# Forgetting attention on one core: cumulative forget terms as stacked high and low rows, three logits banks, longer lags

## The reference, cut to what matters

```python
def forgetting_attention(h, w_in, b_f, w_out):          # 256 tokens, 16 heads of 64
    q, k, v, f_logit = split(h @ w_in)
    log_f = log_sigmoid(f_logit + b_f)                  # one value for each token and head
    c = cumsum(log_f, axis=1)                           # the forget sums
    logits = einsum(q, k) * scale + c[query] - c[key]
    p = softmax(where(key <= query, logits, -inf))      # query blocks of 128
    return einsum(p, v) @ w_out
```

## Time and profile before

| | |
|---|---|
| time, median of 3 runs | 2557.5 us (2547.1 to 2561.46) |
| the profiled execution | 2556.97 us |
| its span | 2555.3 us |
| PE busy / weight loads | 2199.8 us (86%) / 1933.2 us (76%) |
| DVE, ACT, POOL busy | 1588.1, 1111.8, 474.7 us |
| granted PE clock, mean | 0.927 |
| chain that ended last, share of PE | 42%; 12% each for L749, L750, L751 |

### The profile page before, as it was taken

How to read it: one execution, slowest core, us unless ns; L and a number is a source line. 1 busy time by engine, 2 the same in 40 slices (tenths; PEclk the granted TensorE clock), 3 DMA queues, 4 the chain that set the end, 5 groups by cost and what they waited for, 6 DMA issues and landing times.

```text
span 2555.3 us, 40376 instructions
## 1 busy us (share of the span) xinstructions
PE 2199.8 (86%) x15366; PEld 1933.2 (76%) x15376; DVE 1588.1 (62%) x2534; ACT 1111.8 (44%) x1624; POOL 474.7 (19%) x328
## 2 busy tenths in 40 slices
PE   5999887688589775876889999889997999899997
PEld 2776565677377565765868999779996999878997
DVE  2876654477468455765555776576667666546665
ACT  3223443576433544674445455224332433445332
POOL 1000001688400015884052021100000000000000
PEclk7998997899789887998999999989998999999999
DMA  6458611799445036996424466455553345323452
GB/s 249 165 205 320 216 58 63 274 344 347 181 148 199 32 116 215 326 322 223 134 98 181 167 217 225 158 196 188 184 186 132 139 174 205 132 100 116 173 186 85
DMA packets 103174, 471.50 MB, mean 185 GB/s; under 512 B 11520, under 2 KB 30208, under 8 KB 66048
## 3 DMA queue, kind: packets, MB, share of 16 engines
q1 hardware_dynamic: 84480, 404.79, 44.7%
q0 software_dynamic: 13232, 44.84, 4.7%
q10 hardware_dynamic: 5328, 20.07, 1.9%
HBM read 412.76 MB, written 54.79 MB: 183 GB/s over the span
## 4 chain that ended last, share of the span: by engine, by line
PE 42%; DVE 6%; ACT 2%; issue 1%; DVEq 1%; SPq 1%; DMA 0%; POOL 0%; ACTq 0%; POOLq 0%
PE bank L749 12%; PE bank L751 12%; PE bank L750 12%; DVE ring_halves L419 2%; ACT high L1402 1%; PE bank L1257 1%; PE bank L1121 1%; PE bank L1234 1%; PE bank L1247 1%; PE bank L1309 1%; PE bank L1290 1%; PE bank L1239 1%; PE bank L800 0%; DVE dring_halves L428 0%; PE bank L1238 0%
## 5 line engine op out<-in xcount | busy, mean ns | idle before, releaser
L749 PE MATMUL bank<-ssdb_halves,high 128*128 128x256 f32 (+1 forms) x2080 | 620.8, 298 | 49.1 <-DVE HT_halves L1934 18.4
L750 PE MATMUL bank<-HT_halves,high 128*128 128x256 f32 (+1 forms) x2096 | 621.9, 297 | 0.0
L751 PE MATMUL bank<-ssdb_halves,ring_halves 128*128 128x256 f32 (+1 forms) x2080 | 618.4, 297 | 0.0
L419 DVE TENSOR_TENSOR ring_halves<-ring,high 128x2048 fp32r<-128x2048 f32 (+1 forms) x230 | 482.3, 2098 | 195.9 <-ACT high L1402 194.3
L1402 ACT CAST high<-ring 128x2048 fp32r<-128x2048 f32 x230 | 437.3, 1903 | 218.5 <-PE bank L751 120.9
L749 PEld LDWEIGHTS bank<-ssdb_halves,high 128*128 128x128 f32 x2080 | 397.8, 191 | 68.6 <-issue 37.7
L750 PEld LDWEIGHTS bank<-HT_halves,high 128*128 128x128 f32 x2096 | 403.3, 192 | 8.9
L751 PEld LDWEIGHTS bank<-ssdb_halves,ring_halves 128*128 128x128 f32 x2080 | 398.2, 191 | 10.1
L419 POOL TENSOR_TENSOR ring_halves<-ring,high 128x1024 fp32r<-128x1024 f32 x66 | 224.7, 3405 | 674.9 <-ACT high L1402 674.9
L428 DVE TENSOR_TENSOR dring_halves<-dring,dhigh 128x1024 fp32r<-128x1024 f32 (+1 forms) x152 | 226.2, 1488 | 160.8 <-ACT dhigh L1408 160.3
L1408 ACT CAST dhigh<-dring 128x1024 fp32r<-128x1024 f32 x152 | 160.4, 1056 | 244.7 <-PE bank L751 244.6
(11 more groups left out here) (440 smaller groups left out, 3970.3 us busy)
## 6 DMA issues: line engine op xcount, KB each, us to landing
ring<-in_ffn SPq DMA_DIRECT2D x88, 1024.0 KB, 5.6
ring<-in_moe SPq DMA_DIRECT2D x64, 1024.0 KB, 7.3
ring<-in_ada SPq DMA_DIRECT2D x48, 1024.0 KB, 6.1
dring<-in_ffn_down SPq DMA_DIRECT2D x88, 512.0 KB, 3.6
dring<-in_moe_down SPq DMA_DIRECT2D x64, 512.0 KB, 4.6
ring<-in_foxin SPq DMA_DIRECT2D x24, 1024.0 KB, 4.9
ring<-in_win SPq DMA_DIRECT2D x22, 1024.0 KB, 8.0
zs_b<-x_slots POOLq DMA_DIRECT2D x32, 512.0 KB, 8.6
```

The lines of the kernel that those rows point to most:

```text
L419: eng.tensor_tensor(low, w, h, ALU.subtract).then_inc(sem(f"low_{engine}"), 1)
L749: mm(o, a[0], b[0], start=first, stop=last and bool(kw), **kw)
L750: mm(o, a[0], b[1], start=False, stop=last and bool(kw), **kw)
L751: return mm(o, a[1], b[0], start=False, stop=last, **kw)
```

## The change: what it does

The forget sums of all heads are computed once for each layer, and then picked by a small product in each head:

- DVE's `forget` no longer splits into `splr`. It zeroes a 128 x 2 x 128 buffer (`spl_wide`) and writes the 16 columns of log_f into it twice, at columns 0 and 32.
- Behind group 20 PE runs three 128-column fp32 products with the triangle `up` and the matrix `one`. Bank 6 then holds the sums of every head as rows: head h in row h and again in row 32 + h.
- ACT (at its step j = 21) copies them rounded to `spl_rows`, 384 columns; DVE (at its step j = 22) replaces rows 32 to 47 by the rest that rounding lost, two subtractions on 16 partitions.
- In each head one product of `spl_rows` with a broadcast column of `head_of` (ones in rows h, 32 + h, 64 + h, 96 + h) puts high plus low sum into all 384 columns. It stands in for the two L1234 products and the L1235 product.
- The logits have three banks (0, 1, 7), `prob` and `stat` three buffers; `probT` still has two. PE's order becomes logits(h), turn(h-2), values(h-3) for h = 0 to 18; DVE's: maxima of h, division of h-1; ACT's: exponentials of h, copy of h-2, output copies of h-3. `logits(h)` waits for the exponentials of h-3.

The diff:

```diff
@@ -348,10 +349,11 @@
...
         vtok = view(zs_b, 0, TB, D)
-        prob = view(wide, 0, 2, 384)
-        probT = view(wide, 768, 2, 384)
-        fx = view(wide, 1536, 6, TB, 16)
-        stat = view(wide, 1536 + 192, 2, 4, 2)
+        prob = view(wide, 0, 3, 384)
+        probT = view(wide, 1152, 2, 384)
+        fx = view(wide, 1920, 6, TB, 16)
+        stat = view(wide, 1920 + 192, 3, 4, 2)
+        spl_wide, spl_rows = view(border, 2600, TB, P), view(border_r, 0, 384)
         r_col = fx[:, 4, 0, 0:TB]
@@ -1201,6 +1203,11 @@
...
                         narrow_turned(("foxf", i_layer), 16, 7, 256, TB).then_inc(*done("f_raw", i_layer))
+                    if j == 20:
+                        pe.wait_ge(*at("f_sp", i_layer))
+                        mm(ps[6][:, 0:P], spl_wide[:, 0, :], up, start=True, stop=True)
+                        mm(ps[6][:, P:T], spl_wide[:, 0, :], one, start=True, stop=False)
+                        mm(ps[6][:, P:T], spl_wide[:, 1, :], up, start=False, stop=True).then_inc(*done("s5_pe", ("spl_rows", i_layer)))
                 forget = lambda bank: bank[:, 0:T], by_column(H2h, H2r, slice(0, T), 0)
@@ -1217,22 +1224,16 @@
...
                         [(("foxf", i_layer), 0, 5, 0, forget), (("foxin", i_layer), 0, 0, 0, groups[0])], after)
-                spl = fx[:, 5, :, :]
-
                 def logits(h):
                     c, q = h // 2, (h % 2) * HD
-                    L = ps[h % 2]
-                    if h >= 2:
-                        pe.wait_ge(*at("prob", (i_layer, h - 2)))
-                    else:
+                    L = ps[(0, 1, 7)[h % 3]]
+                    if h >= 3:
+                        pe.wait_ge(*at("prob", (i_layer, h - 3)))
+                    elif h == 0:
                         pe.wait_ge(*at("v_sb", (i_layer, 9)))
                         pe.wait_ge(*at(*fox_taken(i_layer, 23)))
-                        pe.wait_ge(*at("f_sp", i_layer))
-
-
-                    for n in range(2):
-                        mm(L[:, 0:384], r(splr[:, n, 0, h:h + 1]).to_broadcast([P, P]), r(fw[:, 0:384]), start=n == 0, stop=True, skip_group_check=True)
-                    mm(L[:, 256:384], spl[:, 1, h:h + 1].to_broadcast([P, P]), up, start=False, stop=True, skip_group_check=True)
+                        pe.wait_ge(*at("s5_dve", ("spl_rows", i_layer)))
+                    mm(L[:, 0:384], r(head_of[:, h:h + 1]).to_broadcast([P, P]), r(spl_rows), start=True, stop=True, skip_group_check=True)
                     diag = L[:].rearrange("p (a m c) -> p a m c", a=2, m=2)[:, :, 0, :]
@@ -1258,13 +1259,13 @@
...
                        start=False, stop=True).then_inc(*done("o", (i_layer, h)))
-                for h in range(FOX_HEADS + 2):
+                for h in range(FOX_HEADS + 3):
                     if h < FOX_HEADS:
                         logits(h)
-                    if 1 <= h <= FOX_HEADS:
-                        turn(h - 1)
-                    if h >= 2:
-                        values(h - 2)
+                    if 2 <= h <= FOX_HEADS + 1:
+                        turn(h - 2)
+                    if h >= 3:
+                        values(h - 3)
                 groups = [(lambda bank: bank[:, 0:T], by_column(H2r, O2r, slice(0, T), j % 2)) for j in range(KC)]
@@ -1763,25 +1764,30 @@
...
                         softplus_log("f", i_layer, fx[:, 3, :, :], fx[:, 1, :, :])
-                for h in range(FOX_HEADS + 2):
-                    p = h % 2
+                    if j == 21:
+                        act.wait_ge(*at("s5_pe", ("spl_rows", i_layer)))
+                        nc.scalar.copy(r(spl_rows[:, 0:T]).rearrange("p (m c) -> p m c", m=2),
+                                       ps[6][:, 0:P].unsqueeze(1).to_broadcast([P, 2, P]))
+                        nc.scalar.copy(r(spl_rows[:, T:]), ps[6][:, P:T]).then_inc(*done("s5_act", ("spl_rows", i_layer)))
+                for h in range(FOX_HEADS + 3):
+                    p = h % 3
                     if h < FOX_HEADS:
                         act.wait_ge(*at("att_max", (i_layer, h)))
-                        if h >= 2:
-                            act.wait_ge(*at("att_turned", (i_layer, h - 2)))
-                        L = ps[p]
+                        if h >= 3:
+                            act.wait_ge(*at("att_turned", (i_layer, h - 3)))
+                        L = ps[(0, 1, 7)[p]]
                         act_fn(prob[:, p, 0:P], L[:, 0:P], ACT.Exp, bias=stat[:, p, 0, 0:1], accum_out=stat[:, p, 1, 0:1])
...
                                accum_out=stat[:, p, 1, 1:2]).then_inc(*done("prob", (i_layer, h)))
-                    if 1 <= h <= FOX_HEADS:
-                        q = (h - 1) % 2
-                        act.wait_ge(*at("att_turned", (i_layer, h - 1)))
-                        if h >= 3:
-                            act.wait_ge(*at("o", (i_layer, h - 3)))
-                        nc.scalar.copy(probT[:, q, :], ps[2 + q][:, 0:384]).then_inc(*done("probT", (i_layer, h - 1)))
-                    if h >= 2 and h % 2 == 1:
-                        c = (h - 2) // 2
-                        act.wait_ge(*at("o", (i_layer, h - 2)))
+                    if 2 <= h <= FOX_HEADS + 1:
+                        q = h % 2
+                        act.wait_ge(*at("att_turned", (i_layer, h - 2)))
+                        if h >= 4:
+                            act.wait_ge(*at("o", (i_layer, h - 4)))
+                        nc.scalar.copy(probT[:, q, :], ps[2 + q][:, 0:384]).then_inc(*done("probT", (i_layer, h - 2)))
+                    if h >= 3 and h % 2 == 0:
+                        c = (h - 3) // 2
+                        act.wait_ge(*at("o", (i_layer, h - 3)))
                         nc.scalar.copy(O2[:, c, :], ps[4 + c % 2][:, 0:T]).then_inc(*done("o_sb", (i_layer, c)))
@@ -2457,6 +2464,13 @@
...
                         forget(i_layer)
+                    if j == 22:
+                        dve.wait_ge(*at("s5_act", ("spl_rows", i_layer)))
+                        low = slice(QUAD, QUAD + 16)
+                        tt(r(spl_rows[low, 0:T]).rearrange("p (m c) -> p m c", m=2),
+                           ps[6][low, 0:P].unsqueeze(1).to_broadcast([16, 2, P]),
+                           spl_rows[low, 0:T].rearrange("p (m c) -> p m c", m=2), ALU.subtract)
+                        tt(r(spl_rows[low, T:]), ps[6][low, P:T], spl_rows[low, T:], ALU.subtract).then_inc(*done("s5_dve", ("spl_rows", i_layer)))
                 attend(i_layer)
@@ -2467,26 +2481,28 @@
...
                          fx[:, 0, :, :], fx[:, 1, :, :], fx[:, 2, :, :], fx[:, 3, :, :], fx[:, 5, :, :], -1.0)
-                dve.drain()
-                nc.vector.tensor_copy(r(splr[:, 0]), fx[:, 5, :, :])
-                dve.drain()
-                tt(r(splr[:, 1]), fx[:, 5, :, :], splr[:, 0], ALU.subtract)
-                dve.drain().then_inc(*done("f_sp", i_layer))
+                tss(spl_wide[:], ident.unsqueeze(1).to_broadcast([P, TB, P]), 0.0, ALU.mult)
+                dve.drain()
+                nc.vector.tensor_copy(spl_wide[:, :, 0:16], fx[:, 5, :, :])
+                nc.vector.tensor_copy(spl_wide[:, :, QUAD:QUAD + 16], fx[:, 5, :, :]).then_inc(*done("f_sp", i_layer))
             def attend(i_layer):
-                for h in range(FOX_HEADS):
-                    p = h % 2
-                    L = ps[p]
-                    dve.wait_ge(*at("att", (i_layer, h)))
-                    nc.vector.reduce_max(stat[:, p, 0, 0:1], L[:, 0:P], AX.X, negate=True)
-                    nc.vector.reduce_max(stat[:, p, 0, 1:2], L[:, P:384], AX.X, negate=True)\
-                        .then_inc(*done("att_max", (i_layer, h)))
-                    dve.wait_ge(*at("prob", (i_layer, h)))
-                    nc.vector.reciprocal(stat[:, p, 2, :], stat[:, p, 1, :])
-                    dve.drain()
-                    tss(prob[:, p, 0:P], prob[:, p, 0:P], stat[:, p, 2, 0:1], ALU.mult)
-                    tss(prob[:, p, P:384], prob[:, p, P:384], stat[:, p, 2, 1:2], ALU.mult)\
-                        .then_inc(*done("prob_n", (i_layer, h)))
+                for h in range(FOX_HEADS + 1):
+                    if h < FOX_HEADS:
+                        p = h % 3
+                        L = ps[(0, 1, 7)[p]]
+                        dve.wait_ge(*at("att", (i_layer, h)))
+                        nc.vector.reduce_max(stat[:, p, 0, 0:1], L[:, 0:P], AX.X, negate=True)
+                        nc.vector.reduce_max(stat[:, p, 0, 1:2], L[:, P:384], AX.X, negate=True)\
+                            .then_inc(*done("att_max", (i_layer, h)))
+                    if h:
+                        p = (h - 1) % 3
+                        dve.wait_ge(*at("prob", (i_layer, h - 1)))
+                        nc.vector.reciprocal(stat[:, p, 2, :], stat[:, p, 1, :])
+                        dve.drain()
+                        tss(prob[:, p, 0:P], prob[:, p, 0:P], stat[:, p, 2, 0:1], ALU.mult)
```

(6 more changed lines are left out.)

## The result

| | median us | runs | lowest to highest |
|---|---|---|---|
| before | 2555.36 | 5 | 2547.1 to 2561.46 |
| changed | 2583.68 | 5 | 2553.92 to 2587.21 |

The ratio of the runs is 1.0099, 95% interval 1.0069 to 1.0128: slower by about 1% where 2539 was forecast. A second set of six runs gave 2583.36 beside 2551.97, ratio 1.0117 (1.0100 to 1.0134). These ratios, and those further down, leave out every run more than 1.5% above the fastest of its kernel (one run of e5; four of e8, whose ratio says little for it); medians and spreads have all runs. The profile of the changed kernel happens to be of its fastest run, 2553.92 us; the second set gives one of a typical run, 2584.23. Both are read here.

What follows compares the result with a forecast made beforehand. PE was taken to bound the steady head loop. Two stages of 7.9 + 0.8 - 0.7 = 8.0 us, plus 0.9 in layer 0, gave 16.9 and 2540; forecast 2539, as some half-clock stretches may go, range 2528 to 2550.

Steps and rivals of the forecast that it cites:

- the shorter head: Attention head loop: one product in a 0.20 us slot replaces three taking 0.68, saving 0.48 us; period 3.00 becomes 2.52.
- The steady loop without waits on PE: Steady heads of both attention stages: PE never waits, with 1.1 us of slack a head.
- the longer lag: PE's order in the head loop: turn(h) after logits(h + 2) gives the serial chain 5.0 us, so PE need not wait.
- the chain of 2.5 us: A head's serial path from maxima through division: would just not fit behind one set of logits at 2.52 us a head.
- all three half-clock stretches as long as now: Both stage starts and layer 0's middle: stretches at clock 0.50 keep their lengths, 10.2 us at starts, 6.9 in the middle.
- The rival "slower": Head loop: small waits in each head drop PE to 1.2 GHz for good; 2607 us if both stages do; chance 0.04.
- busy 30.00 of 30.00: Steady heads before the change: PE busy 30.00 of 30.00 us at clock 1.00, taken as evidence against the slower case.
- the third logits in the gap and the end: Stage start and end: three logits, not two, before the first turn; the end gains 0.8 us a stage (0 to 1.2).
- one or more half-clock stretches go: Attention stages: shorter gaps remove stretches at clock 0.50; 2535 with one gone, about 2527 with all; chance 0.33.
- The start: Each attention stage up to its first turn: gain 7.9 us a stage, idle gap from 2.62 to 2.4 us.
- ACT's and DVE's new steps: Copies and subtractions before the first logits: fit into idle time; if ACT were late, logits late by up to 0.4 us.
- Beside POOL's work: Middle of layer 0's stage: PE idles 2.6 us in place of 3.54; gain 0.9, between -2.7 and +3.5.

Runs made afterwards that it cites:

- e5: The changed kernel with one more 384-column triangle product in each head, result unread: median 2554.92 us, ratio 0.9994 to the kernel before.
- e8: The kernel with old products and longer lag, minus the low part's triangle product in each head: median 2562.29 us, ratio 0.9961 to the kernel before.
- e9: The kernel before with 11 products of zeros ahead of each stage's first turn, where PE idled: median 2542.23 us, ratio 0.9960.
- e7: The changed kernel with each head's single product streaming the constant triangle in place of the stacked rows: median 2574.22 us, ratio 1.0089 to the kernel before.

## Why the prediction was wrong

- The mechanism of the shorter head was right and small: slot 0.28 us, not the 0.20 I took (bounds 0.17 to 0.29), period 2.61, not 2.52. Over 32 heads that is 2.9 us less than forecast. My reason for 0.20, the short bf16 weight load behind it, doesn't hold: in e5 the same product before the same load takes 0.18 behind a triangle product (1301.18 to 1301.36), so what stands ahead of it counts.
- The steady loop without waits on PE was right: 10.00 of 10.00 us busy at 2.4 GHz in layer 0, 47.00 of 47.00 at 1.2 in layer 3. But the longer lag wasn't needed for it: the product alone, with the old lag, has 23.50 of 23.50 us busy at 2.61 us a head, where I had put the chain of 2.5 us as just not fitting.
- **The step that failed** is in the sum: "with all three half-clock stretches as long as now". I read the clock's falls as the effect of idle gaps alone, asked only whether the gaps would grow, and took the length of a stretch as given. For the loop of before the gaps were the cause (e9). In the changed kernel the clock falls with PE at work, in all four profiled stages 2.7 to 2.9 us after the first logits begin, and the loop with less PE work then stays at 1.2 GHz for 23.9 and 61.4 us (68.3 and 68.2 in the typical run) in place of 10.2, with no gap behind the first turn. A fall out of the running loop is not in the record.
- The rival "slower" had the right place, clock and sign (its price was 25 us a stage; measured are 26.1 for both, with the lag's gain inside; a head at half clock takes 4.74 us, 1.8 times the 2.61, and not the 5.0 I took). It had 0.04 because I tied it to a small wait in each head and set "busy 30.00 of 30.00" against it. There are no such waits. The busy share was evidence for nothing here: it reads the same at both levels.
- The lag was under-valued. I gave it the third logits in the gap and the end; measured alone it gives 20.8 us, since the gaps of 2.62 and 2.41 shrink to 1.0 and 0.55 and the three stretches at 1.2 GHz go. Of the first rival, "one or more half-clock stretches go", this is the full case; the product turned it round.
- The start: the gap before the first turn was 1.11 us, not 2.4, in part because the third logits ran at 1.2 GHz. ACT's and DVE's new steps don't hold up the first logits: PE's wait ahead of them is 0.56 us, as before. Beside POOL's work PE idled 0.24 us in layer 0, not 2.6: the upper bound of that term, no stall left, is what came.
- The rule on cycling PSUM banks that I weighed (the Trainium skill, "TensorE: Matmul & The Clock Gate", "A second HAM failure mode: psum-queue depth-cycling") tells of small idles between groups of products and a clock that swings. This case differs: the loop has no idles (47.00 of 47.00 us busy) and its clock stays down. The banks were not the cause: the product-only kernel with two banks falls, the lag-only one with three does not.

## What to carry to other kernels

Before you take products out of a loop that PE paces, write down its period at both clock levels (here 2.61 and 4.74 us against 3.00) and ask what happens if the clock falls at the loop's start: the shorter loop may not get the upper level back. Test with filler products, since zeros serve. First look for idle gaps in front of each half-clock stretch: a deeper pipeline (one more bank and one more buffer) or fillers in the gap were worth 21 and 12 us here, with no arithmetic removed. A kernel on the edge shows itself by its spread (2529 to 2592 for one program), so profile a typical run, not the fastest, and compare the stages that you changed: the rest of this program alone varied by 13.5 us from profile to profile.

## What the hardware showed that I had not expected

- PE's granted clock stayed at 1.2 GHz for 61 to 68 us while the records show it busy without a gap (61.40 of 61.40 us in e7, 68.30 of 68.30 in e8); every stretch over 50 us lasted to within 6 us of its stage's end.
- Two zero products of 0.21 us in each head made the kernel 46 us faster (2583.4 to 2536.8; from 31 us slower than the kernel before to 16 us faster).
- What exactly keeps the clock down stays open. With heads of 2.61 us it is back after 13.7 to 71.7 us; with one triangle product more after 41 and 44; with one zero product, which makes a shorter head, after 6.8 and 10.2; with two products it is back after 6.8 us or doesn't fall. Why layer 0 came back to 2.4 GHz after 23.9 us in one run and not in another was not found.
